# The last output projection: 256-column products, and moving operands read pairwise or by parity

## What is computed

```python
def sublayer(h_res, j, fn, res_w):
    h = rms_norm_2(h_res, norm_g[l, 2 * j]) * (1.0 + scale) + shift
    y = rms_norm_2(fn(h), norm_g[l, 2 * j + 1])
    return h_res + res_w * gate * y
...
def mixer(h):
    z = h @ w_mix_in[l]
    ...
    attn = diff_attention(q, k, v, lam, subln_g[l], lambda_init, cos, sin)
    rec = recurrent_group(xr, yr, conv_w[l], conv_b[l], lru_w_gate[l], lru_b_gate[l], lru_lambda[l])
    return jnp.concatenate([attn, rec], axis=-1) @ w_mix_out[l]

x = sublayer(x, 0, lambda h: swiglu(h, ffn1_w_in[l], ffn1_w_out[l]), 0.5)
x = sublayer(x, 1, mixer, 1.0)
x = sublayer(x, 2, lambda h: swiglu(h, ffn2_w_in[l], ffn2_w_out[l]), 0.5)
```

## Time and profile before

| what | us |
|---|---|
| median of 3 runs | 2518.57 |
| lowest, highest | 2518.31, 2520.13 |
| the profiled execution, its own time | 2519.4 |
| its span, first to last instruction | 2517.5 |
| PE busy | 2445.7 (97%) |
| DVE busy | 1422.5 (57%) |
| ACT busy | 1049.1 (42%) |

### The profile page before, as it was taken

The page is one execution under the profiler, slowest core; times in us unless marked ns, Lnnn a source line. Parts: engine busy times, 40 slices in busy tenths (PEclk is TensorE's granted clock), DMA queues, the critical chain, the costliest instruction groups (busy, mean ns, idle before and its releaser), DMA issues.

```text
span 2517.5 us, 30734 instructions
## 1 busy us (share of the span) xinstructions
PE 2445.7 (97%) x11230; PEld 1970.3 (78%) x11230; DVE 1422.5 (57%) x2065; ACT 1049.1 (42%) x1572; POOL 0.2 (0%) x4
## 2 busy tenths in 40 slices
PE   7899999999999999999999999999989988999999
PEld 6788888878888886888888878888866666888886
DVE  6766666657556567857556564323354775433333
ACT  5555555534223237843223332222346554332233
POOL 0000000000000000000000000000000000000000
PEclk9999999999999999999999999999989999999999
DMA  4222222224444431024534422332311112223231
GB/s 155 68 76 75 75 75 75 76 93 167 142 144 157 161 107 59 1 101 142 168 119 164 159 88 95 100 96 92 104 59 59 50 47 72 80 97 109 84 109 67
DMA packets 71244, 249.55 MB, mean 99 GB/s; under 512 B 9824, under 2 KB 10336, under 8 KB 70752
## 3 DMA queue, kind: packets, MB, share of 16 engines
q1 hardware_dynamic: 68912, 247.28, 29.6%
q10 hardware_dynamic: 2224, 0.79, 0.1%
HBM read 245.94 MB, written 2.10 MB: 99 GB/s over the span
## 4 chain that ended last, share of the span: by engine, by line
PE 92%; DVE 4%; ACT 2%; issue 1%; DMA 0%; SPq 0%; ACTq 0%; DVEq 0%
PE psum L426 27%; PE psum L428 27%; PE psum L427 27%; PE psum L477 2%; PE psum L830 1%; PE psum L508 1%; PE psum L530 1%; PE psum L537 1%; PE psum L881 1%; PE psum L911 0%; PE psum L452 0%; DVE w_lo L1667 0%; PE psum L931 0%; PE psum L513 0%; PE psum L495 0%
## 5 line engine op out<-in xcount | busy, mean ns | idle before, releaser
L426 PE MATMUL psum<-h_hi,w_hi 128*128 128x512 f32 x1768 | 703.5, 398 | 16.9 <-DVE h_lo L1637 11.9
L428 PE MATMUL psum<-h_hi,w_lo 128*128 128x512 f32 x1768 | 692.6, 392 | 0.0
L427 PE MATMUL psum<-h_lo,w_hi 128*128 128x512 f32 x1768 | 692.5, 392 | 0.0
L1011 ACT ACTIVATE w_hi<-raw 128x1024 fp32r<-128x1024 f32 x385 | 404.2, 1054 | 500.6 <-PE psum L428 491.2
L1667 DVE TENSOR_TENSOR w_lo<-raw,w_hi 128x1024 fp32r<-128x1024 f32 x385 | 466.0, 1220 | 157.9 <-ACT w_hi L1011 156.1
L426 PEld LDWEIGHTS psum<-h_hi,w_hi 128*128 128x128 f32 x1768 | 334.9, 189 | 92.3 <-issue 21.2
L428 PEld LDWEIGHTS psum<-h_hi,w_lo 128*128 128x128 f32 x1768 | 334.4, 189 | 71.2
L427 PEld LDWEIGHTS psum<-h_lo,w_hi 128*128 128x128 f32 x1768 | 334.7, 189 | 70.0 <-issue 2.4
L2156 DVE TENSOR_TENSOR s_s<-s_g,psum 128x512 f32<-128x512 f32 x44 | 30.3, 688 | 304.1 <-issue 241.0
L426 PE MATMUL psum<-f_hi,w_hi 128*128 128x512 f32 x512 | 199.2, 389 | 0.0
L427 PE MATMUL psum<-f_lo,w_hi 128*128 128x512 f32 x512 | 199.2, 389 | 0.0
(11 more groups left out here) (340 smaller groups left out, 3231.7 us busy)
## 6 DMA issues: line engine op xcount, KB each, us to landing
raw<-stream SPq DMA_DIRECT2D x385, 512.0 KB, 3.5
ada_raw<-ada_in SPq DMA_DIRECT2D x72, 512.0 KB, 4.0
x<-x_in SPq DMA_DIRECT2D x2, 1024.0 KB, 6.7
out<-x SPq DMA_DIRECT2D x8, 256.0 KB, 2.4
a_mask<-mask_in SPq DMA_DIRECT2D x1, 1024.0 KB, 9.7
crow<-crow_in SPq DMA_DIRECT2D x2, 512.0 KB, 5.4
gatew<-gate_in ACTq DMA_DIRECT2D x2, 256.0 KB, 3.7
a_cos<-rope_in SPq DMA_DIRECT2D x1, 256.0 KB, 8.0
```

Source lines behind the costliest of these rows:

```text
L426: nc.tensor.matmul(o, whi, xh, start=start, stop=False)
L427: nc.tensor.matmul(o, whi, xl, start=False, stop=False)
L428: return nc.tensor.matmul(o, wlo, xh, start=False, stop=stop)
L1011: A(w_hi[:, slot(u0), :], raw[:, slot(u0), :], ACT.Copy).then_inc(S["hi"], 1)
```

## The change

Only units 2 to 7 of this projection are written in another way.

- **Units 2 and 3**: each product of 512 columns becomes two of 256 columns, on the left and the right half of the tokens, one right after the other, each with its own weight load. The first of the two starts the bank's accumulation.
- **Units 4 and 5**: the products keep 512 columns, but the moving operand is read as column 0, 256, 1, 257, 2, 258 and so on (`paired`): alternately from the left and the right half, 1 KB apart. The bank then holds the tokens in that order, and DVE's copy reads it with a step of two columns, to bring them back.
- **Units 6 and 7**: the moving operand is read by parity (`strided`): the 256 even columns, each 8 bytes from the one before, and then the 256 odd ones. DVE's copy reads the bank in order and writes `y` with a step of two columns.

Units 0 and 1, the waits, the banks and the weights stay as they are.

```diff
-            outward(U_MO, mixed_hi, mixed_lo, mixed_ready, mixed_free, "Y", 1, b0=2)
+            def halves(o, whi, wlo, xh, xl, start, stop):
+                for w, m in ((whi, xh), (whi, xl), (wlo, xh)):
+                    for c in (slice(0, T // 2), slice(T // 2, T)):
+                        last = nc.tensor.matmul(o[:, c], w, m[:, c], start=start and w is whi and m is xh and c.start == 0,
+                                                stop=stop and w is wlo, skip_group_check=True)
+                return last
+            def paired(m):
+                return m.rearrange("p (a b) -> p b a", a=2)
+            def strided(m):
+                return m.rearrange("p (b a) -> p a b", a=2)
+            pe.wait_ge(*mixed_free(1))
+            unit_pair(U_MO, (slot(U_MO), slot(U_MO + 1)), (bank(2), bank(3)), mixed_hi, mixed_lo, mixed_ready)
+            for o in range(2, KT):
+                u = U_MO + o
+                pe.wait_ge(*mixed_free(o))
+                pe.wait_ge(*after("lo", u))
+                for k in range(KT):
+                    whi, wlo = tile_of(w_hi, slot(u), k), tile_of(w_lo, slot(u), k)
+                    xh, xl = mixed_hi[:, k, :], mixed_lo[:, k, :]
+                    if o < 4:
+                        last = halves(bank((o + 2) % 4), whi, wlo, xh, xl, k == 0, k == KT - 1)
+                    else:
+                        order = paired if o < 6 else strided
+                        last = mm3(bank((o + 2) % 4), whi, wlo, order(xh), order(xl), k == 0, k == KT - 1)
+                last.then_inc(S["mm"], 1)
+            collected_sums("Y", 1)
...
-                V.tensor_copy(y[:, o, :], bank((o + 2) % 4)).then_inc(S["MO_y"], 1)
+                two = "p (b a) -> p a b"
+                if o < 4:
+                    V.tensor_copy(y[:, o, :], bank((o + 2) % 4)).then_inc(S["MO_y"], 1)
+                elif o < 6:
+                    V.tensor_copy(y[:, o, :].rearrange("p (a b) -> p a b", a=2), bank((o + 2) % 4).rearrange(two, a=2)) \
+                     .then_inc(S["MO_y"], 1)
+                else:
+                    V.tensor_copy(y[:, o, :].rearrange(two, a=2), bank((o + 2) % 4).rearrange("p (a b) -> p a b", a=2)) \
+                     .then_inc(S["MO_y"], 1)
```

## The result

| | us |
|---|---|
| before, median of 5 runs | 2519.11 |
| changed, median of 5 runs | 2529.94 |
| ratio, 95% interval | 1.0043 (1.0028 to 1.0057) |
| the changed kernel's profiled execution, its span | 2530.18, 2528.3 |

A forecast was written before the change was run, and what follows sets the result against it. PE's pace was taken to bound the kernel. Halves 0, pairwise +32.6, parity +10.9 and copies and clock 0 gave +43.5 us, from the median 2518.6 to 2562.1 us (+1.7%); range 2526 to 2568 us.

The forecast's parts named there:

- What bounds: Whole kernel: PE busy 97% of the span; in units 2 to 7 of this projection only PE's pace counts.
- The step that failed: Moving operand reads: each visit to a 16-byte line costs 1.77 ns and serves all neighbouring columns taken in a row.
- the 13.9 ns over twice the clock's pace: Natural-order products of 512 columns: 226.7 ns against 212.8, half the lower level's time; reading the moving operand was a candidate.
- Units 4 and 5: 48 pairwise products, each column a visit: 906 ns instead of 226.7, +32.6 us.
- its lower bound of +0: Units 4 and 5: no cost if the reader holds both lines while alternating, leaving 128 visits.
- Units 6 and 7: 48 products by parity, each line visited twice: 453 ns a product, +10.9 us; bounds +0 and +32.6.
- Units 2 and 3: 96 half-width products at 113 ns each: 0 taken, bounds 0.2 us gained to 0.7 us lost.
- The weight loads: Units 2 and 3, twice as many loads: earlier rows show them 111 ns apart, so each fits under 113 ns.
- The copies and the clock: DVE's copies hidden, unit 7's between 0 and 0.38 us; a clock fall at most 2 us; both taken as 0.
- the lower level's 425.6 ns: Product time at clock 0.50; below 453 and 906, so a clock fall would cost the six units nothing.
- The first rival: Units 4 to 7: one order only, at half pace, the other free; +10.9 us, 2529.5 us, chance 25%.
- two lines are held: First rival's second way: visits cost 1.77 ns, but two held lines make pairs free and parity costs 10.9 us.

The follow-up runs named there:

- widths: Changed kernel with units 2, 3 natural in 384 and 128 columns, 4, 5 pairwise halves, 6, 7 natural halves: 285, 224, 240 ns per 512 columns.
- orders_c: Changed kernel with units 2, 3 reading every fourth column, 4, 5 two parity streams, 6, 7 eight places: 460, 228, 488 ns a product.

## Why the prediction was wrong, point by point

**What bounds: right.** The projection is bound by PE's pace from end to end, and the new paces of six units moved the span by just what they add up to: 0.6 - 0.5 + 10.8 = 10.9 us by units, 10.8 in the span.

**The step that failed** is the one that set the rule: "a visit to a line of 16 bytes costs 1.77 ns, and one visit serves all neighbouring columns taken from it in a row". Two rows were read as one fact. DVE's and ACT's 1.7 to 1.9 ns at 16-byte steps are real, and PE shows the like once every other column of a product steps by 16 bytes (451 ns for 2 x 256 columns, 1.76 each). PE's 1.77 ns a line in natural order is a coincidence: the 13.9 ns over twice the clock's pace were taken as the reading of 128 lines, and (widths) they are 13.3 ns for each product, whatever its width. One measured pace can't tell a cost per column from a cost per product; it takes two widths, and before the change there was only one.

**Units 4 and 5: the wrong term, +32.6 us forecast, -0.5 measured.** The prediction took 906 ns a product, one visit of 1.77 ns for every column, and 215.8 ns was measured, below even its lower bound of +0. The rule had one reader that sees every hop. What the orders fit best is two readers that take columns by turns, each of which then has its own adjacent stream:

| order of the product | one reader gets | ns for 512 |
|---|---|---|
| pairwise, 16 B to 1 KB apart | 0, 1, 2, 3 | 215.8 |
| natural | 0, 2, 4, 6 | 226.7 |
| two parity streams | 0, 2, 4, 6 | 228 |
| 0, 2, 1, 3 | 0, 1, 4, 5 | 227 |
| runs of 4, 32 B apart | 0, 2, 8, 10 | 234 |
| runs of 4, two halves | 0, 2, 256, 258 | 250 |
| four places near, far | 0, 8, 1, 9; 0, 256, 1, 257 | 269, 283 |
| runs of 2, two halves | 0, 256, 2, 258 | 340 |
| every eighth | 0, 16, 32 | 430 |
| parity | 0, 4, 8 | 451 |
| adjacent pairs, 16 B apart | 0, 4, 8 | 453 |
| two streams of every fourth | 0, 4, 8 | 453 |
| every fourth | 0, 8, 16 | 460 |
| eight places | 0, 128, 256, 384, 1 | 488 |

Where one reader takes two or more columns in a row from the same 16 bytes, a product stays between 216 and 250 ns; where each column of a reader is in other 16 bytes than the one before, and a line comes back only in a later pass, it is 430 to 460; orders in which a reader comes back to a line after a hop lie between, and eight places just above. "Advanced Engine Details and Errata", section SBUF Cachelines, of the Trainium skill asks for at least two hits on a line of 16 bytes; counted for the whole product, as the prediction counted it, that would have made parity free, which it isn't at 451 ns. Counted for one reader it parts the 216 to 250 ns from the 430 to 460, but it has no size for what lies between. The rule of its "Vector Engine (DVE) Microarchitecture Reference", section 5.2, that runs of two adjacent words are enough, is stated there for DVE's ports and does not hold for PE: adjacent pairs 16 bytes apart took 453 ns. Nor did single words cost DVE's own copy anything where it writes `y` in steps of 8 bytes: 692 ns against 688.

**Units 6 and 7: 453 forecast, 451 measured, with a wrong picture.** The forecast was 256 visits in one queue, what the runs bear out is 256 columns for each of two readers at about 1.73 ns. For parity both come to the same number, so that it was hit is luck. They part at every fourth column (orders_c), where the forecast's picture has 512 visits and 906 ns, and 460 was measured.

**Units 2 and 3: inside their bounds, the other end of them.** 0 was taken, 0.7 us was the upper bound "if the 13.9 ns belong to each product whatever its width", and 0.6 was measured, for that reason. The weight loads cost nothing at 120 ns, as the earlier trace rows said.

**The copies and the clock: right.** Unit 7's copy took 692 ns, and the granted clock was 1.00 from unit 2 to unit 7. One argument was loose: the prediction says that the six units would lose nothing at the lower level's 425.6 ns, but that holds only for products slower than that. Units 2 to 5, at 239.8 and 215.8 ns, would have lost time. The case didn't arise.

**The chances.** The first rival had the time of 2529.5 us with 25%, by two ways: pairs half as fast with parity free, or pairs free and parity at 453. The second way is what happened, nearly; "two lines are held" was the nearest thought to two readers. The text gave it one sentence there and the lower bound of units 4 and 5, but no weight of its own, and looked for nothing that would have told one reader from two.

**What stays open.** No row shows a reader; the two are inferred from paces. A single reader that takes the columns two at a time, and pays when the two lie in other lines than the two before, would fit the same rows as well, and no run here tells them apart. What is shown is that the pace goes by where every other column lies. The paces of 250 to 340 ns, where a reader alternates between places, fit no single number, nor do the 488 ns of eight places and the 430 of every eighth column. Why a product costs 13.3 ns over the clock's pace in natural order and 2.5 (215.8 - 213.3, which is 512 columns at 2.4 GHz) pairwise isn't explained either. Only fp32r products with 128 x 128 weights were tried.

## To carry to other kernels

Where PE bounds and its moving operand is 4 bytes wide, try reading it pairwise from two places, "p (a b) -> p b a" with a = 2, and undo the order when PSUM is read: it was worth 10.9 of 226.7 ns for each product of 512 fp32r columns, 3.7% of this whole kernel. Don't let every other column of a product step steadily by 16 bytes or more: 430 to 460 instead of 227 ns. Before a cost is called one per column or one per product, measure it at two widths.

## What the runs showed of the hardware that I had not expected

- A moving operand that hops for every column can be faster than an adjacent one: 215.8 ns against 226.7 for 512 fp32r columns at a granted clock of 1.00, at distances of 16, 64, 256 and 1024 bytes alike.
- PE's pace goes by every other column of a product. Two streams with 8-byte steps cost 228 ns together and two with 16-byte steps 453; one stream of adjacent pairs 16 bytes apart costs 453 too.
- At 16-byte steps DVE and ACT take 1.7 to 1.9 ns a column, and each of PE's readers, if there are two, 1.73 to 1.77.
- In the streams read here weight loads of 128 x 128 follow one another at no steady pace under about 111 ns, with products of 128 columns as with pairwise ones of 256 (112 ns).
- DVE and ACT read PSUM, and DVE writes SBUF, in 8-byte steps at full pace: 691, 596 and 692 ns for 512 columns.
